# The reciprocal root of a layer norm's variance: one GpSimd power in place of a ScalarE root and a VectorE reciprocal

## The chip, the cores and the metric

The kernel runs on one core of a Trainium2 chip. The metric is the device time of one execution in microseconds. Five engines have instruction streams of their own: TensorE (PE, matmuls), VectorE (DVE), ScalarE (ACT), GpSimd (POOL) and SyncE (SP), which issues nearly all DMAs. Within a stream the order is fixed; between streams the program orders work by semaphores that one instruction raises and another waits for.

## What is computed

The kernel is a two-layer decoder trunk on 256 tokens of width 1024, in float32. Each layer is a token mixer followed by a channel mixer (dense in layer 0, 8 experts with top 2 in layer 1). The change is in the token mixer, in the layer norm of its convolution branch:

```python
def layer_norm(x, g, b):
    mu = jnp.mean(xf, axis=-1, keepdims=True)
    xc = xf - mu
    var = jnp.mean(xc * xc, axis=-1, keepdims=True)
    y = xc * lax.rsqrt(var + LN_EPS) * g + b

def conformer_conv(a, b, dw, dw_b, ln_g, ln_b, w_conv_out):
    u = a * jax.nn.sigmoid(b)
    u = depthwise_conv(u, dw, 31 taps, causal) + dw_b
    u = jax.nn.silu(layer_norm(u, ln_g, ln_b))
    return u @ w_conv_out

def hybrid_mixer(...):
    proj = h @ w_in
    a, b, p, gc, gp = split(proj)
    merged = sigmoid(gc) * conformer_conv(a, b, ...) + sigmoid(gp) * multiscale_pool(p, ...)
    return merged @ w_out
```

The layer norm runs over 512 channels, once in each of the two layers.

## The kernel before

**Weights.** All weights stream from memory in units of 128x2048 float32 (1 MB) into a ring (`raw`). A unit is split for the matmuls into a high part by ScalarE (`w_hi`, L511) and a low part by VectorE (`w_lo`, L765), into three buffers each; a product is three matmuls, high by high (L1108), low by high (L1109) and high by low (L1110). ScalarE may split unit n only when TensorE has finished unit n-3 (`unit_used`). The helper `split_to(n)` puts all splits below n at that place of the engine's stream; U is the first unit of the layer.

**The convolution branch.** It is held transposed, channels on partitions and 256 tokens along a row: `conv` is 128 x (4 chunks x 256), a part of `work`. VectorE and GpSimd sum the 31 taps; GpSimd's additions are the loop over `ADDS` (L450). TensorE then makes the mean over channels by four matmul groups with `mean_w` (L1222), so that every partition holds the mean of each token. VectorE subtracts it (L842), ScalarE squares (L602), and TensorE makes the variance in `bank[7]` (L1228), placed amid the first half of the unit U+12. From there:

- ScalarE takes the square root of variance plus epsilon, 128x256, into `ln_std` (L605).
- VectorE takes the reciprocal into `ln_rstd` (L846) and multiplies all four chunks of `conv` by it (L847), which raises `normed`.
- ScalarE splits unit U+15 and, once `normed` is up, makes for each chunk a sigmoid and an affine map (L610, L611), and after them the fourth block of gate sigmoids (`gate_half(U, 3)`, L552). VectorE multiplies (L852) for the silu, ScalarE and VectorE split the result into `cT_hi` and `cT_lo` (L615, L855).

**TensorE meanwhile** goes through units U+12 and U+13 (gate columns), then the pooling product with unit U+14 for token block 1, and for token block 0 after it, which waits for the gate sigmoids of L552 because they still occupy its banks. Then come the convolution's output product (units U+15, U+16), a transpose, and the output projection.

**GpSimd meanwhile** multiplies the gate block `gate_p` by a row of gains (L459): the two of the left half right after its additions, the two of the right half once L552 has written them. VectorE needs all four (`gate_p_scaled`, L863). In layer 1 the constants of the router follow on GpSimd. It also makes the reciprocal roots of the RMS norms, by a power of a 128x2 tile with the exponent -0.5 held in `small[:, 4:6]` (L402), and of 128x1 tiles at the end (L468).

`ln_std` and `ln_rstd` are halves of the tile `sq`, which the trace calls `work`.

Of the kernel before, what the change touches and what calls it, by code (L numbers as in the profile page):

```python
# [7 lines left out]
ALU = mybir.AluOpType  # L8
ACT = mybir.ActivationFunctionType
# [5 lines left out]
P = 128  # L15
UNIT = 2048
RAW = 7
RMS_EPS, LN_EPS = 1e-6, 1e-5
# [27 lines left out]
def trunk_kernel(nc, x, mix_norm, w_in, conv_dw, conv_dw_b, conv_ln_g, conv_ln_b, w_conv_out, w_pool, pool_scale,  # L46
                 w_out, ffn_norm, dense_w_gate, dense_w_up, dense_w_down, router_w, moe_w_gate, moe_w_up,
                 moe_w_down, final_norm, out):
    _, S, D = x.shape
# [119 lines left out]
    with ExitStack() as ctx:  # L169
        def sb(name, shape, dt=F32):  # L170
            return ctx.enter_context(nc.sbuf_tensor(name, shape, dt))

        def sem(name):
            return ctx.enter_context(nc.semaphore(name))
# [3 lines left out]
        small = sb("small", [P, 16])  # L178
# [79 lines left out]
        ln_std, ln_rstd = sq[:, 0:S], sq[:, S:2 * S]  # L258
# [7 lines left out]
        bank = [ctx.enter_context(nc.psum_tensor(f"bank{i}", [P, N], F32)) for i in range(8)]  # L266
# [21 lines left out]
        prod_ready, prod_added, diag_ready, pe_taps_done = sem("prod_ready"), sem("prod_added"), sem("diag_ready"), sem("pe_taps_done")  # L288
        pooled_done, dT_hi_ready, dT_ready = sem("pooled_done"), sem("dT_hi_ready"), sem("dT_ready")
        mean_done, centred, centred_sq, var_done = sem("mean_done"), sem("centred"), sem("centred_sq"), sem("var_done")  # L290
        std_ready, normed, sig_conv, silu_conv = sem("std_ready"), sem("normed"), sem("sig_conv"), sem("silu_conv")
        cT_hi_ready, cT_ready = sem("cT_hi_ready"), sem("cT_ready")
        yp_merged, yc_gated, merged_ready = sem("yp_merged"), sem("yc_gated"), sem("merged_ready")
# [84 lines left out]
        @block.gpsimd  # L378
        def _(pool):
            seen = Seen(PER_ITEM)  # L380
            steps = [0]

            def step(ins):

                steps[0] += 1
                ins.then_inc(pool_step, 1)
                pool.wait_ge(pool_step, steps[0])


            step(pool.memset(ident[:, :], 0.0))  # L390
            step(pool.affine_select(out=ident[:, :], in_=ident[:, :], compare_op=ALU.not_equal, fill=1.0, base=0,
                                    pattern=[[-1, P]], channel_multiplier=1))
            pool.memset(small[:, 4:6], -0.5)
            pool.memset(small[:, 13:14], LN_EPS)
            pool.memset(uT[:, :, 0:PAD], 0.0)
            step(pool.memset(mean_w[:, :], 1.0 / CD))
            pool.memset(small[:, 12:13], 0.0).then_inc(consts_ready, 1)

            def inverse_root():

                pool.wait_ge(meansq_ready, seen.next(meansq_ready))
                pool.tensor_tensor(small[:, 6:8], small[:, 2:4], small[:, 4:6], ALU.pow).then_inc(rstd_ready, 1)  # L402

            def tap_diagonals(l):
                for j in range(TP):
                    ins = pool.tensor_scalar(diag[:, j, :], ident[:, :], taps[:, l, CC * j + 2:CC * j + 3], None, ALU.mult)  # L406
                ins.then_inc(diag_ready, 1)

            pool.wait_ge(taps_ready, L)
            tap_diagonals(0)  # L410
            inverse_root()

            for g, w in enumerate(WINDOWS):
                pool.memset(band_0[:, g, w - 1:], 1.0 / w)
                for t in range(w - 1):
                    pool.memset(band_0[:, g, t:t + 1], 1.0 / (t + 1))
                step(pool.memset(band_1[:, g, :], 1.0 / w))
                for band, cols in ((band_0, P + REACH), (band_1, P)):
                    step(pool.affine_select(out=band[:, g, :], in_=band[:, g, :], compare_op=ALU.is_ge, fill=0.0, base=0,
                                            pattern=[[1, cols]], channel_multiplier=-1))  # L420
                    step(pool.affine_select(out=band[:, g, :], in_=band[:, g, :], compare_op=ALU.is_ge, fill=0.0,
                                            base=w - 1, pattern=[[-1, cols]], channel_multiplier=1))
                    step(pool.tensor_tensor(band[:, g, 0:P], band[:, g, 0:P], ident[:, :], ALU.subtract))  # L423
            pool.memset(small[:, 12:13], 0.0).then_inc(consts_ready, 1)

            def router_constants():

                step(pool.memset(ones[:, :], 1.0))
                step(pool.affine_select(out=before[:, :], in_=ones[:, :], compare_op=ALU.is_gt, fill=0.0, base=0,
                                        pattern=[[1, P]], channel_multiplier=-1))  # L430
                step(pool.iota(slot_int[:, :], pattern=[[1, P]], base=0, channel_multiplier=0))
                step(pool.tensor_copy(slot_no[:, :], slot_int[:, :]))
                for e in range(E):
                    pool.memset(rev[:, :, e:e + 1], float(E - e))
                    pool.memset(expert[:, e:e + 1], float(e))
                    if e:
                        pool.memset(earlier[:, e, 0:e], 1.0)
                    pool.memset(earlier[:, e, e:E], 0.0)
                pool.memset(slot_of[:, :], NOWHERE)
                step(pool.memset(comb_of[:, :], 0.0))  # L440
                pool.memset(small[:, 12:13], 0.0).then_inc(consts_ready, 1)

            for l in range(L):

                for c, first, n, before_this in ADDS:
                    pool.wait_ge(prod_ready, len(PRODUCTS) * l + n + 1)
                    if before_this:
                        pool.wait_ge(prod_added, len(ADDS) * l + before_this)
                    part = conv[:, c, :] if first is None else tap_prod[:, (len(PRODUCTS) * l + first) % PRODS, :]
                    pool.tensor_tensor(conv[:, c, :], part, tap_prod[:, (len(PRODUCTS) * l + n) % PRODS, :],  # L450
                                       ALU.add).then_inc(prod_added, 1)

                pool.wait_ge(gain_landed, seen.next(gain_landed, 16))
                pool.wait_ge(gates_ready, seen.next(gates_ready, 2 * TB))
                for h in range(2):
                    for b in range(TB):
                        pool.wait_ge(gates_ready, seen.next(gates_ready))
                        part = gate_p[:, b, h * N:(h + 1) * N]
                        pool.tensor_tensor(part, part, row_gain[:, h * N:(h + 1) * N], ALU.mult).then_inc(gate_p_scaled, 1)  # L459
                if l == L - 1:  # L460
                    router_constants()
                inverse_root()
                if l == 0:
                    tap_diagonals(1)
                    inverse_root()
            for b in range(TB):
                pool.wait_ge(meansq_ready, seen.next(meansq_ready))
                pool.tensor_tensor(small[:, 6 + b:7 + b], small[:, 2 + b:3 + b], small[:, 4 + b:5 + b],  # L468
                                   ALU.pow).then_inc(rstd_ready, 1)
# [28 lines left out]
        def _(act):  # L498
            seen = Seen(PER_ITEM)
            unit = [0]  # L500

            def split_to(n):

                while unit[0] < n:
                    u = unit[0]
                    slot, landed, _ = where(u, seen.item is not None)
                    act.wait_ge(raw_landed[slot], seen.at(raw_landed[slot], landed))
                    if u >= SPLIT:
                        act.wait_ge(unit_used, seen.at(unit_used, u - SPLIT + 1))
                    width = unit_width(u)  # L510
                    act.activation(w_hi[:, u % SPLIT, 0:width], place[slot][:, 0:width], ACT.Copy).then_inc(hi_ready, 1)  # L511
                    unit[0] += 1
# [42 lines left out]
            def mixer(l, U):  # L555
# [45 lines left out]
                act.wait_ge(centred, seen.next(centred))  # L601
                act.activation(sq, work[:, 0, :], ACT.Square).then_inc(centred_sq, 1)  # L602
                split_to(U + 15)
                act.wait_ge(var_done, seen.next(var_done))
                act.activation(ln_std[:, :], bank[7][:, 0:S], ACT.Sqrt, bias=small[:, 13:14]).then_inc(std_ready, 1)  # L605
                split_to(U + 16)
                act.wait_ge(normed, seen.next(normed))
                for c in range(CC):
# [138 lines left out]
        def _(dve):  # L747
            seen = Seen(PER_ITEM)
# [3 lines left out]
            def step(ins):  # L752

                steps[0] += 1
                ins.then_inc(dve_step, 1)
                dve.wait_ge(dve_step, steps[0])
# [51 lines left out]
            def mixer(l, U):  # L808
# [27 lines left out]
                bias = vecs[:, V_CB + CC * l + 2:V_CB + CC * l + 3]  # L836
# [5 lines left out]
                dve.tensor_tensor(conv[:, :, :], conv[:, :, :], bank[6][:, 0:S].unsqueeze(1).to_broadcast([P, CC, S]),  # L842
                                  ALU.subtract).then_inc(centred, 1)
                split_to(U + 15)
                dve.wait_ge(std_ready, seen.next(std_ready))
                step(dve.reciprocal(ln_rstd[:, :], ln_std[:, :]))  # L846
                dve.tensor_tensor(conv[:, :, :], conv[:, :, :], ln_rstd[:, :].unsqueeze(1).to_broadcast([P, CC, S]),  # L847
                                  ALU.mult).then_inc(normed, 1)
                split_to(U + 16)
# [570 lines left out]
```

## Time and profile before

| | before |
|---|---|
| device time, median of three runs | 1507.9 us (1507.87 to 1508.37) |
| the profiled execution's device time | 1507.77 us |
| its span in the trace | 1506.0 us |
| layer 0's token mixer | about the first 158 us |
| layer 1's token mixer | about 330 to 485 us |
| TensorE busy | 97% of the span |
| VectorE busy | 79% |
| ScalarE busy | 66% |
| GpSimd busy | 10% |

The span is the time from the first to the last instruction in the trace; the device time of that execution is 1.8 us more. A row of the page's list of groups names a line, an engine, the tiles written and read, their shapes and the count, then the busy time, the mean duration of one and the idle time of the engine just before them. A row of a timeline gives the start in the span, the duration, and in brackets how long the engine was idle before and what ended that.

### The profile page before, as it was taken

The numbers are of one execution on the slowest core, as the hardware profiler recorded it, in microseconds if no ns is written. First come the engines' busy times: TensorE is split into PE (matmuls) and PEld (weight loads), VectorE is DVE, ScalarE is ACT, GpSimd is POOL, SyncE is SP. The second block draws the span as 40 slices with busy tenths as digits, with TensorE's granted clock in tenths as the row PEclk, the third lists the DMA queues.
The fourth block names the chain that finished last, engine by engine and source line by source line (L and its number), as shares of the span: only waits on it lengthen the run. The fifth ranks groups of instructions, "written<-read, shape, count | busy, mean of one in ns | idle before, by whom it ended". The sixth has DMA issues, their size and how long they took to land.

```text
span 1506.0 us, 18439 instructions
## 1 busy us (share of the span) xinstructions
PE 1458.6 (97%) x6617; PEld 1200.0 (80%) x6617; DVE 1193.4 (79%) x979; ACT 993.0 (66%) x880; POOL 152.0 (10%) x236
## 2 busy tenths in 40 slices
PE   7989999999989899999999999999999999999997
PEld 5877888888867688888888888878888888888885
DVE  4767554455867798998899899899889889889986
ACT  5665534435764577767777777776777777777764
POOL 6860400000760000000000000000000000000000
PEclk9999999999999799999999999999999999999999
DMA  9445555555336489999899899998988989999890
GB/s 351 158 139 181 184 182 195 189 175 193 123 117 238 173 324 394 345 341 379 339 357 365 335 364 356 356 385 328 385 346 338 383 333 365 357 356 382 332 369 29
DMA packets 186224, 434.42 MB, mean 288 GB/s; under 512 B 7825, under 2 KB 11201, under 8 KB 186177
## 3 DMA queue, kind: packets, MB, share of 16 engines
q1 hardware_dynamic: 184704, 432.20, 77.1%
q10 hardware_dynamic: 1472, 1.61, 0.3%
q8 instruction: 28, 0.46, 0.1%
q14 instruction: 20, 0.16, 0.0%
HBM read 432.73 MB, written 1.05 MB: 288 GB/s over the span
## 4 chain that ended last, share of the span: by engine, by line
PE 81%; POOL 6%; DVE 4%; issue 4%; ACT 3%; DMA 0%; POOLq 0%; SPq 0%; DVEq 0%; ACTq 0%
PE bank L1108 25%; PE bank L1110 25%; PE bank L1109 25%; POOL work L450 4%; PE bank L1257 2%; ACT w_hi L511 2%; DVE w_lo L765 2%; POOL gates L406 1%; DVE dT_lo L1032 1%; PE bank L1328 1%; PE bank L1353 1%; POOL mix L423 1%; PE bank L1354 0%; DVE xs L892 0%; PE bank L1336 0%
## 5 line engine op out<-in xcount | busy, mean ns | idle before, releaser
L765 DVE TENSOR_TENSOR w_lo<-raw,w_hi 128x2048 fp32r<-128x2048 f32 x315 | 716.9, 2286 | 241.6 <-ACT w_hi L511 240.7
L511 ACT ACTIVATE w_hi<-raw 128x2048 fp32r<-128x2048 f32 x315 | 602.5, 1918 | 361.2 <-PE bank L1110 354.3
L1108 PE MATMUL bank<-w_hi,dT_hi 128*128 128x512 f32 (+1 forms) x912 | 360.7, 395 | 8.2 <-DVE w_lo L765 3.7
L1110 PE MATMUL bank<-w_hi,dT_lo 128*128 128x512 f32 (+1 forms) x912 | 355.0, 389 | 0.0
L1109 PE MATMUL bank<-w_lo,dT_hi 128*128 128x512 f32 (+1 forms) x912 | 354.6, 389 | 0.0
L1108 PE MATMUL bank<-w_hi,cT_hi 128*128 128x512 f32 x568 | 223.4, 393 | 0.0
L1110 PE MATMUL bank<-w_hi,cT_lo 128*128 128x512 f32 x568 | 221.3, 390 | 0.0
L1109 PE MATMUL bank<-w_lo,cT_hi 128*128 128x512 f32 x568 | 221.1, 389 | 0.0
L1108 PEld LDWEIGHTS bank<-w_hi,dT_hi 128*128 128x128 f32 x912 | 172.0, 189 | 47.9 <-issue 6.6
L1110 PEld LDWEIGHTS bank<-w_hi,dT_lo 128*128 128x128 f32 x912 | 171.8, 188 | 36.2
L1109 PEld LDWEIGHTS bank<-w_lo,dT_hi 128*128 128x128 f32 x912 | 172.0, 189 | 33.5
L1108 PE MATMUL bank<-w_hi,hT_hi 128*128 128x512 f32 x464 | 184.7, 398 | 0.7 <-DVE hT_lo L782 0.7
L1109 PE MATMUL bank<-w_lo,hT_hi 128*128 128x512 f32 x464 | 181.9, 392 | 0.0
L1110 PE MATMUL bank<-w_hi,hT_lo 128*128 128x512 f32 x464 | 181.9, 392 | 0.0
L1110 PEld LDWEIGHTS bank<-w_hi,cT_lo 128*128 128x128 f32 x568 | 106.6, 188 | 22.4
L1109 PEld LDWEIGHTS bank<-w_lo,cT_hi 128*128 128x128 f32 x568 | 106.7, 188 | 21.5
L1108 PEld LDWEIGHTS bank<-w_hi,cT_hi 128*128 128x128 f32 x568 | 106.7, 188 | 21.3
L468 POOL TENSOR_TENSOR small<-small 128x1 f32<-128x1 f32 x2 | 2.1, 1036 | 1010.0 <-DVE small L1095 1010.0
L1108 PEld LDWEIGHTS bank<-w_hi,hT_hi 128*128 128x128 f32 x464 | 88.1, 190 | 19.1 <-DVE w_lo L765 1.0
L1110 PEld LDWEIGHTS bank<-w_hi,hT_lo 128*128 128x128 f32 x464 | 87.9, 189 | 18.7
L1109 PEld LDWEIGHTS bank<-w_lo,hT_hi 128*128 128x128 f32 x464 | 88.0, 190 | 18.0
L765 DVE TENSOR_TENSOR w_lo<-work,w_hi 128x2048 fp32r<-128x2048 f32 x32 | 73.4, 2292 | 11.9 <-ACT w_hi L511 11.9
(189 smaller groups left out, 1282.9 us busy)
## 6 DMA issues: line engine op xcount, KB each, us to landing
raw<-in_moe_w_gate_dram SPq DMA_DIRECT2D x96, 1024.0 KB, 7.0
raw<-in_moe_w_up_dram SPq DMA_DIRECT2D x72, 1024.0 KB, 8.7
raw<-in_moe_w_down_dram SPq DMA_DIRECT2D x72, 1024.0 KB, 7.3
raw<-in_w_in_dram SPq DMA_DIRECT2D x28, 1024.0 KB, 5.3
mix<-in_moe_w_up_dram SPq DMA_DIRECT2D x16, 1024.0 KB, 8.8
gates<-in_moe_w_down_dram SPq DMA_DIRECT2D x16, 1024.0 KB, 9.4
gates<-in_moe_w_up_dram SPq DMA_DIRECT2D x16, 1024.0 KB, 9.0
work<-in_moe_w_down_dram SPq DMA_DIRECT2D x16, 1024.0 KB, 9.3
```

The costliest lines, as they stand in the source:

```text
L406: ins = pool.tensor_scalar(diag[:, j, :], ident[:, :], taps[:, l, CC * j + 2:CC * j + 3], None, ALU.mult)
L423: step(pool.tensor_tensor(band[:, g, 0:P], band[:, g, 0:P], ident[:, :], ALU.subtract))
L450: pool.tensor_tensor(conv[:, c, :], part, tap_prod[:, (len(PRODUCTS) * l + n) % PRODS, :], ALU.add).then_inc(prod_added, 1)
L511: act.activation(w_hi[:, u % SPLIT, 0:width], place[slot][:, 0:width], ACT.Copy).then_inc(hi_ready, 1)
L765: dve.tensor_tensor(w_lo[:, u % SPLIT, 0:width], place[slot][:, 0:width], w_hi[:, u % SPLIT, 0:width].bitcast(F32), ALU.subtract).then_inc ...
L1032: dve.scalar_tensor_tensor(tokT_lo[:, k, :], bank[6 + k // 4][:, (k % 4) * P:(k % 4 + 1) * P], vecs[:, g:g + 1], tokT_hi[:, k, :].bitcast( ...
L1108: nc.tensor.matmul(dst, a_hi, b_hi, start=start, stop=False)
L1109: nc.tensor.matmul(dst, a_hi, b_lo, start=False, stop=False)
L1110: return nc.tensor.matmul(dst, a_lo, b_hi, start=False, stop=stop)
L1257: last = nc.tensor.transpose(bank[banks + b][:, f * P:(f + 1) * P], tokP[:, b, f * P:(f + 1) * P], ident[:, :])
L1328: last = nc.tensor.matmul(bank[6 + h][:, :], onehot[:, b, :], part[:, b, h * N:(h + 1) * N], start=b == 0 and part is xn_hi, stop=b == TB ...
L1353: nc.tensor.matmul(bank[banks[h]][:, :], spreadT[:, b, :], y_hi[:, part], start=True, stop=False)
```

## The change

ScalarE's root (L605) goes. VectorE's reciprocal goes as well; in its place VectorE adds epsilon to the variance while it reads it from the bank, and waits. GpSimd, after its additions and before its gate multiplications, raises the 128x256 result to the power -0.5, the exponent read from one column of `small` for all 256 elements. A new semaphore, `ln_root_ready`, tells VectorE to go on with the multiplication.

```diff
@@ gpsimd, in the loop over layers, behind the additions
+                pool.wait_ge(std_ready, seen.next(std_ready))
+                pool.tensor_tensor(ln_rstd[:, :], ln_std[:, :], small[:, 4:5].to_broadcast([P, S]), ALU.pow).then_inc(ln_root_ready, 1)
 
                 pool.wait_ge(gain_landed, seen.next(gain_landed, 16))
                 pool.wait_ge(gates_ready, seen.next(gates_ready, 2 * TB))
@@ scalar
                 split_to(U + 15)
-                act.wait_ge(var_done, seen.next(var_done))
-                act.activation(ln_std[:, :], bank[7][:, 0:S], ACT.Sqrt, bias=small[:, 13:14]).then_inc(std_ready, 1)
                 split_to(U + 16)
@@ vector
                 split_to(U + 15)
-                dve.wait_ge(std_ready, seen.next(std_ready))
-                step(dve.reciprocal(ln_rstd[:, :], ln_std[:, :]))
+                dve.wait_ge(var_done, seen.next(var_done))
+                dve.tensor_scalar(ln_std[:, :], bank[7][:, 0:S], LN_EPS, None, ALU.add).then_inc(std_ready, 1)
+                dve.wait_ge(ln_root_ready, seen.next(ln_root_ready))
                 dve.tensor_tensor(conv[:, :, :], conv[:, :, :], ln_rstd[:, :].unsqueeze(1).to_broadcast([P, CC, S]),
                                   ALU.mult).then_inc(normed, 1)
```

ScalarE's stream from the square (`work<-work 128x1024`) to the sigmoids of layer 0; a table load is an instruction by which the engine fetches the function that the next one uses. Before:

```order
51 L602 ACTIVATE work<-work 128x1024 [waits centred]
52 L511 ACTIVATE w_hi<-raw 128x1024 [waits unit_used,raw_landed0]
53 L605 ACT_TABLE_LOAD
54 L605 ACTIVATE work<-bank,small 128x256 [waits var_done]
55 L511 ACTIVATE w_hi<-raw 128x2048 [waits unit_used,raw_landed1]
56 L610 ACT_TABLE_LOAD
57 L610 ACTIVATE work<-work,vecs 128x256 [waits normed]
58 L611 ACTIVATE work<-work,vecs 128x256
```

And now:

```order
51 L606 ACTIVATE work<-work 128x1024 [waits centred]
52 L515 ACTIVATE w_hi<-raw 128x1024 [waits unit_used,raw_landed0]
53 L515 ACTIVATE w_hi<-raw 128x2048 [waits unit_used,raw_landed1]
54 L612 ACTIVATE work<-work,vecs 128x256 [waits normed]
55 L613 ACTIVATE work<-work,vecs 128x256
```

The root and both table loads beside it are gone, in both layers.

GpSimd's stream behind the additions of layer 0. Before:

```order
57 L450 TENSOR_TENSOR work<-work,tap_prod 128x256 [waits prod_added,prod_ready] x38
58 L459 TENSOR_TENSOR gates<-gates,row_gain 128x512 [waits gates_ready,gain_landed]
59 L459 TENSOR_TENSOR gates<-gates,row_gain 128x512 [waits gates_ready] x3
60 L402 TENSOR_TENSOR small<-small 128x2 [waits meansq_ready]
61 L406 TENSOR_SCALAR gates<-ident,taps 128x128 x16
```

And now:

```order
57 L451 TENSOR_TENSOR work<-work,tap_prod 128x256 [waits prod_added,prod_ready] x38
58 L455 TENSOR_TENSOR work<-work,small 128x256 [waits std_ready]
59 L463 TENSOR_TENSOR gates<-gates,row_gain 128x512 [waits gates_ready,gain_landed]
60 L463 TENSOR_TENSOR gates<-gates,row_gain 128x512 [waits gates_ready] x3
61 L403 TENSOR_TENSOR small<-small 128x2 [waits meansq_ready]
62 L407 TENSOR_SCALAR gates<-ident,taps 128x128 x16
```

The power is one more instruction, ahead of all four gate multiplications. VectorE's stream keeps its length: the reciprocal's place is taken by the addition of epsilon.

## Rows read from the trace of the kernel before

**Rows 1.** The page's first part: busy time, share of span, instructions.
```profile
PE 1458.6 (97%) x6617; PEld 1200.0 (80%) x6617; DVE 1193.4 (79%) x979; ACT 993.0 (66%) x880; POOL 152.0 (10%) x236
```
**Rows 2.** The page's chain that ended last, by engine.
```profile
PE 81%; POOL 6%; DVE 4%; issue 4%; ACT 3%; DMA 0%; POOLq 0%; SPq 0%; DVEq 0%; ACTq 0%
```
**Rows 3.** That chain in order of time, 104 to 120: start, us, what.
```profile
105.25 1.73 PE bank L1228 x8
...
109.81 1.92 ACT w_hi L511
111.73 0.02 issue
111.75 1.28 ACT L610
113.03 0.01 issue
113.04 0.60 ACT work L610
...
117.09 1.16 ACT gates L552 x2
118.24 0.04 issue
118.29 0.39 PE bank L1108
```
**Rows 4.** ACT's timeline, layer 0: start, us, instruction, idle before and its end.
```profile
105.32 1.28 ACT L605 ACT_TABLE_LOAD   x1
107.02 0.48 ACT L605 ACTIVATE work<-bank,small 128x256 f32<-128x256 f32 x1 [0.42 <-PE bank L1228]
```
**Rows 5.** DVE's timeline over the same stretch.
```profile
107.53 1.75 DVE L846 RECIPROCAL work<-work 128x256 f32<-128x256 f32 x1 [0.97 <-ACT work L605]
109.31 1.22 DVE L847 TENSOR_TENSOR work<-work 128x1024 f32<-128x1024 f32 x1
111.76 2.29 DVE L765 TENSOR_TENSOR w_lo<-raw,w_hi 128x2048 fp32r<-128x2048 f32 x1 [1.22 <-ACT w_hi L511]
```
**Rows 6.** PE's timeline: the variance, and the pooling product's two blocks.
```profile
105.09 1.89 PE L1228 MATMUL bank<-work,mean_w 128*128 128x256 f32 x8
...
116.30 0.28 PE L1110 MATMUL bank<-w_hi,dT_lo 128*128 128x256 f32 x1
118.29 0.39 PE L1108 MATMUL bank<-w_hi,dT_hi 128*128 128x256 f32 x1 [1.70 <-ACT gates L552]
```
**Rows 7.** ACT's timeline at the same place of layer 1.
```profile
434.11 0.47 ACT L605 ACTIVATE work<-bank,small 128x256 f32<-128x256 f32 x1
...
440.07 0.60 ACT L610 ACTIVATE work<-work,vecs 128x256 f32<-128x256 f32 x1
```
**Rows 8.** Groups by shape on POOL: shapes, count, busy us, mean ns, idle.
```profile
L450 POOL TENSOR_TENSOR work<-tap_prod 128x256 f32<-128x256 f32 x4 | 2.9, 733 | 25.4 <-ACT tap_prod L543 25.4
L402 POOL TENSOR_TENSOR small<-small 128x2 f32<-128x2 f32 x4 | 2.9, 720 | 252.2 <-DVE small L774 252.2
```
**Rows 9.** The lines of the two powers: duration ns min/median/max.
```profile
L402 POOL TENSOR_TENSOR small<-small x4: 712/718/732, 30.7 to 488.8; 128x2 f32<-128x2 f32 x4
...
L468 POOL TENSOR_TENSOR small<-small x2: 547/1036/1526, 1498.8 to 1500.1; 128x1 f32<-128x1 f32 x2
```
**Rows 10.** The timeline at the kernel's end, the two 128x1 powers.
```profile
1498.84 0.55 POOL L468 TENSOR_TENSOR small<-small 128x1 f32<-128x1 f32 x1 [1009.31 <-DVE small L1095]
...
1499.91 1.27 DVE L1098 SCALAR_TENSOR_TENSOR xs<-xs,small,row_gain 128x1024 f32<-128x1024 f32 x1
1500.07 1.53 POOL L468 TENSOR_TENSOR small<-small 128x1 f32<-128x1 f32 x1 [0.69 <-DVE small L1095]
```
**Rows 11.** POOL's timeline: a 128x2 power and what runs behind it.
```profile
164.53 0.71 POOL L402 TENSOR_TENSOR small<-small 128x2 f32<-128x2 f32 x1 [44.07 <-DVE small L774]
165.22 4.88 POOL L406 TENSOR_SCALAR gates<-ident,taps 128x128 f32<-128x128 f32 x5
```
**Rows 12.** DVE, by line: a 128x256 tensor_scalar that reads a bank.
```profile
L934 DVE TENSOR_SCALAR work<-bank,vecs x4: 475/480/483, 484.7 to 486.3; 128x256 f32<-128x256 f32 x4
```
**Rows 13.** Stretches: length, then PE, PEld, DVE, ACT, POOL busy, PEclk, DMA share, GB/s.
```profile
503.90:509.00 5.10, 5.09 (x12) 4.04 (x13) 2.86 (x9) 1.16 (x3) 0.00 (x0) 0.50 0.63 206
509.00:514.00 5.00, 5.00 (x23) 4.09 (x23) 2.29 (x1) 3.77 (x2) 0.00 (x0) 0.99 0.00 0
```
**Rows 14.** POOL's timeline: the gate multiplications of layer 0.
```profile
100.69 2.50 POOL L459 TENSOR_TENSOR gates<-gates,row_gain 128x512 f32<-128x512 f32 x2
117.74 2.72 POOL L459 TENSOR_TENSOR gates<-gates,row_gain 128x512 f32<-128x512 f32 x2 [14.55 <-ACT gates L552]
```

More of the change, by code:

```diff
@@ L290, in trunk_kernel @@
         mean_done, centred, centred_sq, var_done = sem("mean_done"), sem("centred"), sem("centred_sq"), sem("var_done")
+        ln_root_ready = sem("ln_root_ready")
         std_ready, normed, sig_conv, silu_conv = sem("std_ready"), sem("normed"), sem("sig_conv"), sem("silu_conv")
```

## The prediction

> **What bounds the kernel now.** I read the busy shares first: TensorE is busy for 97% of the span, GpSimd for 10% [rows 1], so a change that does not alter what TensorE does can cost or gain only where TensorE waits. The chain that ended last agrees, with 81% on TensorE and only 3% on ScalarE [rows 2]. The question is therefore whether the root, the reciprocal and the power lie on the chain at the place where they stand. I read the chain in order of time there [rows 3]. It goes from the variance over TensorE's own products to ScalarE's split of the next unit (109.81), then a table load (111.75, 1.28 us), eight sigmoids and affine maps (from 113.04), the gate sigmoids (until 118.25), and back to TensorE at 118.29, which had stood idle for 1.70 us [rows 6]. The root and the reciprocal are not in it. The timelines say why: the root ran from 107.02 to 107.50 [rows 4], the reciprocal from 107.53 to 109.28, the multiplication from 109.31 to 110.53 [rows 5], while ScalarE could not use the result before 113.04. The branch that is changed has 113.04 - 110.53 = 2.51 us of slack. Layer 1 shows the same, from the root at 434.11 to the first sigmoid at 440.07 [rows 7].
>
> **What is removed.** ScalarE loses the root (0.48 us) and two table loads of 1.28 us each. The first load and the root stand where ScalarE would wait anyway, since the split that follows them waits for TensorE until 109.81 [rows 3]. The second load, 111.75 to 113.03, is on the chain. Without it the sigmoids can begin at 111.75, if `normed` is up by then. So the whole removal is worth at most 113.04 - 111.75 = 1.29 us a layer, and TensorE's idle 1.70 us at 118.29 has room for it. Two layers: 2.6 us. VectorE loses the reciprocal, 1.75 us, which hid in the slack.
>
> **What is added on VectorE.** One 128x256 addition that reads a bank. The nearest row is a tensor_scalar of that shape that reads a bank, 0.48 us [rows 12]. The variance is complete at 105.09 + 1.89 = 106.98 [rows 6], so the addition runs until about 107.50, when the root ended before. It costs nothing itself. Queued behind the new wait on VectorE are the multiplication, the split of unit U+15 (2.29 us) and the silu products; the split has its input from 111.73 on and TensorE needs it only behind the stall, so the wait costs what the power costs, once.
>
> **What is added on GpSimd: the term that decides.** The power can begin at about 107.58, when the engine has long finished its left gate multiplications in the old order and, in the new, its additions. Its duration T at 128x256 is not in the trace. The bounds are these. A plain addition of 128x256 takes 0.73 us [rows 8]; a power cannot well be cheaper, so that is the low end. The trace has the same operation at two tiny widths: 128x2 takes 712 to 732 ns, median 718, in four instances, and 128x1 takes 547 ns [rows 9]. The other 128x1 power shows 1.53 us, but it ran against a VectorE instruction with two SBUF inputs from 1499.91 to 1501.18 [rows 10], so I take the undisturbed one. These numbers carry much for their size: two elements of power cost nearly what 256 elements of addition cost. The second element costs 718 - 547 = 171 ns, and 547 - 171 = 376 ns are fixed. If each further element costs as much, T = 547 + 255 x 171 ns = 44.2 us. If nothing were fixed, the highest reading would be 256 x 547 ns = 140 us, which the 128x2 rows already contradict; with the 128x2 row taken as two equal elements behind some 0.13 us of start, (718 - 130) / 2 = 294 ns an element gives 75 us. (The 0.13 us is my estimate of a GpSimd instruction's bare cost from two rows: 0.73 us for an addition of 256 elements and 1.25 us, half of 2.50, for a product of 512 [rows 8, 14], so about 2.0 ns an element and 0.2 us or less fixed.) I take 44.2 us, since both rows of the same operation lie on that line and no row shows a power at a lower price per element.
>
> The Trainium skill, page Perfetto Trace Analysis, section GPSIMD Engine Instruction, says that a GpSimd span in a profile is unreliable and that one should go by the distance between starts. Here the instruction behind a 128x2 power starts 165.22 - 164.53 = 0.69 us after it [rows 11], so at least these rows hold.
>
> **The sum.** The power ends at 107.58 + 44.2 = 151.8. VectorE multiplies for 1.22 us, until 153.05, and ScalarE starts its sigmoids at about 153.1 in place of 113.04: +40.0 us in layer 0. The split of unit U+15 now runs behind the multiplication on VectorE, 2.29 us, while ScalarE is already at the sigmoids; the silu products then start 2.3 us after the sigmoids do, and catch up by the time ScalarE reaches `cT_hi` (4.05 + 1.16 us after the first sigmoid, by rows 3), so nothing is added there. GpSimd's left gate multiplications move from 100.69 to behind the power; they take 2.5 us [rows 14], and the right pair waits for the gate sigmoids 5.2 us after the first sigmoid, as now. No cost. TensorE stands idle from about 116.6 to 158.3. Its granted clock falls in such a pause: after the idle stretch of the router, 12 matmuls of 512 columns took 5.1 us at 0.50, that is at 1.2 GHz, and then 23 took 5.0 us at 0.99 [rows 13]. That costs 5.1 - 12 x 5.0/23 = 2.5 us there; I take 2.3, with 0 and 2.5 as bounds, as the first products here are only 256 columns wide and the one TensorE idle row that I have at this very place, 1.70 us, shows no drop. The removed table load is already in the 40.0. Layer 0: 42.3. Layer 1 has the same distances, root 434.11 and sigmoid 440.07 against 107.02 and 113.04 [rows 7], so 42.3 again. Together +84.6 us on the span of 1506.0: 1590.6, and with the 1.8 us that the device time lies above the span, 1592.4. The median of the runs, 1507.9, is 0.1 above the profiled 1507.77, so I say 1592.5.
>
> Nothing gives this back later. The stall lets the ring of weights fill, but TensorE is the bound behind it, not the DMAs; the seven units are full after a few microseconds, and then SyncE stops too, because VectorE frees no unit while it waits.
>
> **Rivals.** (A) The power is cheap in bulk: the first elements pay a start that the rest do not, and each further element costs what an addition's does, T = 0.73 to 1.2 us. Then `normed` is up at about 110.1, the sigmoids start at 111.75, and each layer gains 1.29 us: 1507.9 - 2.6 = 1505.3, not slower. The point from which this decides is exact: `normed` must be up by 113.04, so the power must end by 113.04 - 1.22 - 0.08 = 111.74, T at most 4.2 us; above it the change loses, below 2.9 us the gain is whole. For it speaks that the trace cannot tell a start from a price per element beyond two elements. Against it: the second element alone cost 171 ns, and under (A) it should have cost a few. The Trainium skill, GPSIMD Engine Reference, section 3.1, gives about 2.6 cycles an element for a two-input operation and about 12 for a body with data-dependent branches; taken as rules for a power they would give 0.6 or 2.6 us by estimate, which is (A). The step between the 128x1 and the 128x2 rows speaks against applying them to a power.
>
> (B) The loop takes several elements at once when it has them, and the tiny tiles see only the remainder path. With four at the price of one, T = 0.4 + 64 x 0.171 = 11.3 us; `normed` at about 120.2, the sigmoids +7.1 us, TensorE idle for 8.8 us and so up to 2.3 us of lower clock: +9.4 a layer, 1507.9 + 18.8 = 1526.7. For it: ordinary in such loops. Against: 128x2 would then rather cost like 128x1 if two were already paired.
>
> (C) The fixed part is smaller than the line says, and the price is the proportional one, T = 75 us: (75 - 4.2) + 2.3 = 73.1 a layer, 1654. For it: only the single undisturbed 128x1 row speaks for 376 ns fixed.
>
> That the change doesn't do what it says is unlikely, as both table loads are gone from the order.
>
> **How the numbers follow.** The forecast 0.62, (B) and what lies between it and the forecast 0.16, (C) 0.12, (A) 0.10. The forecast's own range is T from 38 to 50 us and 0 to 2.5 us for the clock, 1575 to 1605. To hold 8 in 10 the range must reach over (B) and toward (C): 1525 to 1654. A measurement of this kernel can tell about 0.2%, 3.0 us, from no change. (A)'s whole gain is 2.6 us and so inside that; faster by more has 0.02. (A) otherwise, and a T of up to 5.7 us that loses at most 1.5 us a layer, make 0.08 for no change. Slower has 0.90.
>
> **What would show it.** The duration of GpSimd's power at 128x256 is the one number to read first: 44 us by me, 11 by (B), 75 by (C), about 1 by (A). Then ScalarE should show no table load at the sigmoids, and idle until the multiplication; TensorE should be idle at the pooling product's second block until the gate sigmoids for some 41.7 us in place of 1.70, in both layers, with a granted clock of about 0.5 behind it for up to 5 us. Busy time of GpSimd should rise from 152 to about 240 us. I would be wrong if the power's price per element is not what two tiny tiles say; all else hangs on it by subtraction.

## The result and the profile after

The changed kernel takes 1588.1 us (median of four runs, 1586.96 to 1588.64) against 1507.9 (1507.16 to 1508.37): ratio 1.0531, 95% interval 1.0513 to 1.0550, so 5.3% slower, +80.2 us. The forecast was 1592.5. Single executions of one kernel lie up to 5 us apart, so differences of a microsecond are read from the traces. The span of the profiled execution grew from 1506.0 to 1586.3.

The page after, first part, and the chain by engine and line, to be held against [rows 1, 2]:

```profile
PE 1463.2 (92%) x6617; PEld 1203.8 (76%) x6617; DVE 1194.1 (75%) x979; ACT 986.9 (62%) x874; POOL 236.2 (15%) x238
...
PE 76%; POOL 11%; issue 5%; DVE 4%; ACT 2%; DMA 0%; POOLq 0%; SPq 0%; DVEq 0%; ACTq 0%
```

TensorE does the same 6617 matmuls in the same busy time but for 4.6 us; what fell is its share. GpSimd has 84.2 us more. All but 2 us of that are two instructions, the line of the power (count, duration in ns, who waited in us):

```profile
L455 POOL TENSOR_TENSOR work<-work,small x2: 41138/41145/41152, 107.9 to 475.7; 128x256 f32<-128x256 f32 x2
...
who waited for it (us, times):
  DVE work L850: 82.5, 2
```

Layer 0's chain in order of time, after, against [rows 3]: the power, the multiplication, the sigmoids, and TensorE again.

```profile
107.94 41.16 POOL work L455
149.10 0.02 issue
149.12 2.29 DVE work L850
151.41 0.02 issue
151.44 0.60 ACT work L612
...
155.48 1.16 ACT gates L556 x2
156.63 0.04 issue
156.68 0.58 PE bank L1111
```

Both of ScalarE's table loads are gone, as the order said. Its split of unit U+15 ends at 112.15, and the engine then stands for 39.3 us. TensorE stands for 39.7 us in each layer, where it stood for 1.70 [rows 6]:

```profile
156.68 0.58 PE L1111 MATMUL bank<-w_hi,dT_hi 128*128 128x256 f32 x1 [39.67 <-ACT gates L556]
...
524.43 0.58 PE L1111 MATMUL bank<-w_hi,dT_hi 128*128 128x256 f32 x1 [39.67 <-ACT gates L556]
```

Where the 80.3 us of span come from can be read from four starts in each layer: VectorE's subtraction of the mean, the first sigmoid, and the last pair of gate products on VectorE (L869 before, L872 after) that wait for TensorE.

| us | before, layer 0 | after | before, layer 1 | after |
|---|---|---|---|---|
| subtraction starts | 102.04 | 101.28 | 429.54 | 470.72 |
| first sigmoid | 113.04 | 151.44 | 440.07 | 519.19 |
| last gate pair | 130.92 | 172.06 | 457.96 | 538.66 |
| subtraction to sigmoid | 11.00 | 50.16 | 10.53 | 48.47 |
| sigmoid to last gate pair | 17.88 | 20.62 | 17.89 | 19.47 |

The first stretch grew by 39.2 and 37.9, the second by 2.7 and 1.6: 81.4 in all. The span grew by 1.1 less: 0.76 us went ahead of layer 0's subtraction and 0.40 behind layer 1's last gate pair. The 1.2 us by which layer 0's first stretch grew more than layer 1's are TensorE's clock ahead of the variance, which stood low for longer in this execution than in the one before: over 4 us from just ahead of the subtraction the granted clock was 0.50 (100.24 to 104.24), and 0.76 before (101 to 105). It has nothing to do with the power behind it: when the same kernel was executed again, the first stretch took 48.47 us in layer 0 and 48.46 in layer 1.

### The profile page after: what moved, and what is told of

It is laid out like the page before. It is cut to its first block, busy times and chain, and to the rows that moved or that the text cites. A ratio compares the mean times of both kernels' runs of the same rounds, so it can differ in the third digit from the quotient of the medians.

```text
span 1586.3 us, 18435 instructions
## 1 busy us (share of the span) xinstructions
PE 1463.2 (92%) x6617; PEld 1203.8 (76%) x6617; DVE 1194.1 (75%) x979; ACT 986.9 (62%) x874; POOL 236.2 (15%) x238
## 4 chain that ended last, share of the span: by engine, by line
PE 76%; POOL 11%; issue 5%; DVE 4%; ACT 2%; DMA 0%; POOLq 0%; SPq 0%; DVEq 0%; ACTq 0%
PE bank L1111 24%; PE bank L1113 24%; PE bank L1112 24%; POOL work L455 5%; POOL work L451 4%; PE bank L1260 2%; DVE w_lo L767 2%; ACT w_hi L515 1%; POOL gates L407 1%; DVE dT_lo L1035 1%; PE bank L1331 1%; PE bank L1356 0%; PE bank L1357 0%; DVE xs L895 0%; POOL mix L420 0%
## 5 line engine op out<-in xcount | busy, mean ns | idle before, releaser
L1111 PE MATMUL bank<-w_hi,dT_hi 128*128 128x512 f32 (+1 forms) x912 | 361.8, 397 | 84.2 <-ACT gates L556 79.3
L455 POOL TENSOR_TENSOR work<-work,small 128x256 f32<-128x256 f32 x2 | 82.3, 41145 | 13.7 <-DVE work L848 13.7
```

The costliest lines, as they stand in the source:

```text
L455: pool.tensor_tensor(ln_rstd[:, :], ln_std[:, :], small[:, 4:5].to_broadcast([P, S]), ALU.pow).then_inc(ln_root_ready, 1)
L1111: nc.tensor.matmul(dst, a_hi, b_hi, start=start, stop=False)
```

## Experiments

### What a power costs by width

The kernel before, with root and reciprocal kept, and one more power of n columns on GpSimd, which VectorE's multiplication waits for. Nobody reads its result.

```diff
                 pool.wait_ge(gain_landed, ...)          # ahead of this line:
+                pool.wait_ge(std_ready, seen.next(std_ready))
+                pool.tensor_tensor(sq[0:128, 2 * S:2 * S + 16], ln_std[0:128, 0:16], small[0:128, 4:5].to_broadcast([128, 16]), ALU.pow).then_inc(ln_root_ready, 1)
...
                 step(dve.reciprocal(ln_rstd[:, :], ln_std[:, :]))
+                dve.wait_ge(ln_root_ready, seen.next(ln_root_ready))
```

> The kernel before, root and reciprocal kept, with one added power of 128x16 on GpSimd (its result goes where nobody reads it) that VectorE's multiplication waits for. By the straight line through 128x1 (0.547 us) and 128x256 (41.145 us), 159 ns an element: 0.547 + 15 x 0.159 = 2.9 us. If the price per element falls with the width: less at 16 than the line for small widths (171 ns an element, 3.1 us) and visibly under it.

> As the run with 16 columns, with 64. By the line: 0.547 + 63 x 0.159 = 10.6 us. The kernel grows by (10.6 - 0.1) us a layer and up to 2.5 for the clock, less the slack of about 2.5 us that before has there: about 1508 + 2 x 9 = 1526.

> As the run with 16 columns, with 128. By the line: 0.547 + 127 x 0.159 = 20.7 us; the kernel then takes about 1508 + 2 x 20 = 1548.

> As the run with 16 columns, with all 256 columns but only 8 of the 128 partitions. If GpSimd raises all partitions of a column together, the power takes 41 us as with 128 partitions. Rival (it goes through the partitions one after another, so that the price is per number and not per column): half or less, 20 us or under.

The line of the power in the four kernels, in this order (ns, least, median, most):

```profile
L455 POOL TENSOR_TENSOR work<-work,small x2: 2904/2911/2918, 107.3 to 435.7; 128x16 f32<-128x16 f32 x2
```
```profile
L455 POOL TENSOR_TENSOR work<-work,small x2: 10532/10538/10545, 108.3 to 445.6; 128x64 f32<-128x64 f32 x2
```
```profile
L455 POOL TENSOR_TENSOR work<-work,small x2: 20737/20744/20751, 107.5 to 454.8; 128x128 f32<-128x128 f32 x2
```
```profile
L455 POOL TENSOR_TENSOR work<-work,small x2: 41127/41134/41140, 106.5 to 474.1; 8x256 f32<-8x256 f32 x2
```

With the 128x256 power's 41145 ns this is a straight line. From 16 to 64 columns a column costs (10538 - 2911) / 48 = 158.9 ns, from 64 to 128 it costs 159.5, from 128 to 256 it costs 159.4. So a power takes about 0.36 us and 159.4 ns a column, with no discount for width: rival (B) is out, and so are (A) and (C). And 256 columns of 8 partitions take 41.134 us, as those of 128 do: with 8 partitions and with 128 the price is that of the row's length. All four durations came out as expected. Every power here has the exponent -0.5; another exponent was not tried.

The kernels took 1509.3, 1527.7, 1546.8 and 1586.3 us (one run each, 1507.2 for before beside them). The step from 16 to 64 columns, 7.6 us of power a layer, is 9.2 us a layer; from 128 to 256 (on 8 partitions), 20.4 us of power, it is 19.8. What the first step has on top is TensorE's clock. With 16 columns TensorE waits for 1.71 us, as before, and the first sigmoid and the last gate pair are 17.89 us apart; with 64 it waits for 9.1 us, and they are 20.63 and 19.29 us apart. With 256 columns, a wait of 39.8 us, they are 20.32 and 19.22 apart. So in these runs the clock's cost is all there at a pause of 9 us, and a longer one added nothing.

### What is left when the power is cheap

The changed kernel with the power replaced by a product; the reciprocal root is left out.

```diff
-pool.tensor_tensor(ln_rstd[:, :], ln_std[:, :], small[:, 4:5].to_broadcast([P, S]), ALU.pow).then_inc(ln_root_ready, 1)
+pool.tensor_tensor(ln_rstd[:, :], ln_std[:, :], small[:, 4:5].to_broadcast([P, S]), ALU.mult).then_inc(ln_root_ready, 1)
```

> The changed kernel with the power replaced by a product of the same shape and operands; the reciprocal root is left out. My theory (all of the loss is the power's own length and what TensorE's clock does behind the pause it makes; the hand-over itself is free): GpSimd's instruction takes about 0.8 us, ScalarE's sigmoids start when its split ends, the two table loads of each layer are gone, 1.29 us a layer is gained: 1505.3 us. Rival (the hand-over from VectorE to GpSimd and back, or the displaced gate multiplications, cost too): above 1508.

1505.95 us against 1507.42, ratio 0.9985 (0.9976 to 0.9994): between 0.9 and 3.6 us faster, with the expected 2.6 inside. ScalarE's timeline in layer 0 shows what the forecast's rival (A) described, sigmoids directly behind the split and no load between; TensorE's wait went from 1.70 to 0.29 us:

```profile
109.90 1.92 ACT L515 ACTIVATE w_hi<-raw 128x2048 fp32r<-128x2048 f32 x1 [5.54 <-PE bank L1113]
111.72 0.58 ACT L612 ACTIVATE work<-work,vecs 128x256 f32<-128x256 f32 x1
```
```profile
116.96 0.38 PE L1111 MATMUL bank<-w_hi,dT_hi 128*128 128x256 f32 x1 [0.29 <-ACT gates L556]
```

So the hand-over to GpSimd and back is free here, and the loss comes with the power's length: the power itself, and what follows from the pause that it makes. The displaced gate multiplications stood beside VectorE's multiplication in this run too, which took 2.29 us, but it was done by 110.53, before ScalarE's split was. The values behind the layer norm are others in this run; the count of TensorE's matmuls, 6617, is the same.

### The order of GpSimd's work behind the power

In the changed kernel VectorE's multiplication took 2.28 us, where it had taken 1.22 [rows 5], and the split behind it 3.35 in place of 2.29. The left gate multiplications, which the power had pushed behind itself, ran beside them, and took 3.47 us in place of 2.50 [rows 14]:

```profile
149.06 3.47 POOL L463 TENSOR_TENSOR gates<-gates,row_gain 128x512 f32<-128x512 f32 x2
```

The experiment puts them back ahead of the power.

```diff
-                pool.wait_ge(std_ready, ...)
-                pool.tensor_tensor(ln_rstd ..., ALU.pow)
                 for h in range(2):
+                    if h == 1:
+                        pool.wait_ge(std_ready, ...)
+                        pool.tensor_tensor(ln_rstd ..., ALU.pow)
                     for b in range(TB):
```

> The changed kernel with the two left gate multiplications put back ahead of the power. In the trace after, VectorE's multiplication took 2.28 us in place of 1.22 while GpSimd ran these products beside it. If they held each other up, the multiplication is 1.22 us again and each layer is 1.06 us shorter: 1588.1 - 2.1 = 1586.0. Rival (the multiplication is slow for another reason, such as reading what the power has just written): stays at 1588.1 and at 2.28 us.

The multiplication and the split, in the changed kernel and in this one:

```profile
149.12 2.28 DVE L850 TENSOR_TENSOR work<-work 128x1024 f32<-128x1024 f32 x1 [41.27 <-POOL work L455]
151.33 3.35 DVE L767 TENSOR_TENSOR w_lo<-raw,w_hi 128x2048 fp32r<-128x2048 f32 x1
```
```profile
149.46 1.23 DVE L851 TENSOR_TENSOR work<-work 128x1024 f32<-128x1024 f32 x1 [41.26 <-POOL work L460]
150.60 2.28 DVE L768 TENSOR_TENSOR w_lo<-raw,w_hi 128x2048 fp32r<-128x2048 f32 x1
```

The mechanism is settled: alone, both are back at their old length, although the multiplication still reads what the power has just written; beside GpSimd's products each was 1.06 us longer. The times fit turns of one instruction each: the first product ended at 150.32 as if alone (1.26 us) and the multiplication 1.08 us later; the second product ended 1.13 us after the multiplication, and the split about 2.1 us after that. The median does not show the gain. This kernel took 1586.34 us against 1507.42 (ratio 1.0514, 1.0500 to 1.0529). For a closer comparison the changed kernel was run again, unedited.

> The changed kernel itself, unedited, beside the others of this call, so that small differences to it can be read on one chip. 1588.1 us, 80.2 above before; the run with the left gate multiplications ahead of the power gave 1586.3 and the one that keeps TensorE busy 1582.8, so if this one comes out at 1587 to 1589 both steps (about 2 and about 4 to 5 us) stand.

It took 1587.02 against 1508.14 (1.0526, 1.0512 to 1.0540), inside the 1587 to 1589 of the expectation. But each time has to be held against the kernel before beside it, and both are 78.9 us above that: the 2.1 us that were expected don't show in the medians, though the intervals leave room for them. The traces show them (us, layer 0 / layer 1):

| stretch | changed kernel | left gates first | changed, again |
|---|---|---|---|
| subtraction to VectorE's addition | 6.15 / 4.47 | 6.27 / 4.97 | 4.46 / 4.47 |
| addition to first sigmoid | 44.01 / 44.00 | 42.94 / 42.94 | 44.01 / 43.99 |
| sigmoid to last gate pair | 20.62 / 19.47 | 19.59 / 20.54 | 19.41 / 20.37 |

The middle row, in which the power and the multiplication lie, is 1.07 and 1.06 us shorter. The other two, with TensorE's clock ahead of the variance and behind the pause, vary by 1 to 2 us with no edit at all, and that is as much as the gain.

### TensorE's clock behind the pause

```diff
                 for b in reversed(range(TB)):
+                    if b == 0:
+                        for _ in range(170):
+                            nc.tensor.matmul(bank[6][:, :], w_hi[:, s, 0:P], w_hi[:, s, 0:N], start=True, stop=True)
                     pe.wait_ge(gates_ready, seen.next(gates_ready, TB))
```

> The changed kernel with 170 products of 512 columns added on TensorE in the pause of each layer, written to a bank whose contents nobody reads any more. They last 170 x 0.227 = 38.6 us of a pause of 39.7. If the lower clock behind the pause is what made the stretch from the first product to the end of the convolution's output product 2.7 us longer in layer 0 and 1.6 us in layer 1, the time falls by 4.3 us: 1583.8. Rival (that stretch is longer for another reason, such as the later splits): stays at 1588.1.

1582.79 us against 1507.42, ratio 1.0495 (1.0481 to 1.0510): 75.4 above before, where the changed kernel is 78.9 to 80.2 above. So 170 needless products in each pause make the kernel 3.5 to 4.8 us faster. The pause ends at 156.68 in the changed kernel's layer 0; here TensorE starts on the product at 154.58, and the sigmoids began 2.1 us earlier too. The stretches tell why the time falls, first of the changed kernel, then of this one (length, busy us of PE, PEld, DVE, ACT and POOL, granted clock, DMA share, GB/s):

```profile
156.00:161.00 5.00, 4.32 (x16) 4.04 (x17) 4.05 (x6) 4.94 (x8) 2.69 (x2) 0.50 0.57 202
161.00:166.00 5.00, 5.00 (x20) 3.99 (x20) 5.00 (x6) 0.62 (x1) 0.00 (x0) 0.83 0.58 175
```
```profile
156.00:161.00 5.00, 5.00 (x25) 4.16 (x24) 5.00 (x6) 3.37 (x2) 0.75 (x1) 1.00 0.22 87
161.00:166.00 5.00, 5.00 (x24) 4.14 (x23) 5.00 (x7) 1.92 (x1) 0.00 (x0) 1.00 0.74 218
```

After the pause TensorE runs at 1.2 GHz; kept busy, it comes out at 2.4. From the first sigmoid (149.33) to the last gate pair (167.22) it now takes 17.89 us, and 17.89 in layer 1, as before the change (17.88 and 17.89), against 20.62 and 19.47.

### A power of 128x2

The variance is made by a product with equal weights, so every partition holds the same 256 values, and the 128x256 power computes each of them 128 times. As a row's length is what costs, the tokens belong on the partitions. TensorE's product is turned round, so that its result is 128x2; GpSimd raises that; VectorE scales the identity by it; and one more product, with `mean_w`, spreads it over all partitions. (Every element of `mean_w` is 1/512; the factor `CD`, 512, makes up for that.)

```diff
-nc.tensor.matmul(bank[7][:, 0:S], mean_w[:, :], sq[:, c * S:(c + 1) * S], ...)
+nc.tensor.matmul(bank[7][:, b:b + 1], sq[:, c * S + b * P:c * S + (b + 1) * P], mean_w[:, 0:1], ...)   # for both b
...
+dve.tensor_scalar(small[:, 8:10], bank[7][:, 0:TB], LN_EPS, None, ALU.add)
+pool.tensor_tensor(small[:, 10:12], small[:, 8:10], small[:, 4:6], ALU.pow)
+dve.tensor_scalar(sq[:, b * P:(b + 1) * P], ident[:, :], small[:, 10 + b:11 + b], float(CD), ALU.mult, ALU.mult)   # for both b
+nc.tensor.matmul(bank[6][:, 0:S], mean_w[:, :], sq[:, 0:S], start=True, stop=True)   # behind the first unit of U+12
 dve.tensor_tensor(conv, conv, bank[6][:, 0:S] for all chunks, ALU.mult)
```

> The same mathematics with a power of 128x2: TensorE makes the variance with tokens on partitions (128x2 in place of 256 tokens repeated on all 128 partitions), VectorE adds epsilon, GpSimd raises 128x2 to -0.5, VectorE scales the identity by it (two of 128x128), and one TensorE product spreads it to all partitions behind the first unit of U+12. My theory: power 0.72 us, normed by about 111.4 in layer 0's time of before, sigmoids at 111.75 with no table load: 1.29 us a layer gained, 1505.3. Rival (the longer chain over five engines' hand-overs is late and eats the load's gain): 1507 to 1510.

1507.12 against 1507.42, ratio 0.9995 (0.9986 to 1.0004): no change, so the rival was right about the time. VectorE's timeline shows what ate the gain, and it isn't the length of the chain:

```profile
107.52 0.16 DVE L849 TENSOR_SCALAR small<-bank 128x2 f32<-128x2 f32 x1 [1.60 <-PE bank L1237]
108.50 2.54 DVE L852 TENSOR_SCALAR work<-ident,small 128x128 f32<-128x128 f32 x2 [0.82 <-POOL small L455]
111.83 1.22 DVE L855 TENSOR_TENSOR work<-work,bank 128x1024 f32<-128x1024 f32 x1 [0.79 <-PE bank L1243]
```

The two diagonal products stood beside GpSimd's left gate multiplications (108.44 to 110.96) and ended only when those did. From VectorE's addition to the first sigmoid it is now 5.57 us, where it had been 6.02 from the root on, and behind the sigmoids each layer is 0.3 us longer, which was not traced further. The same two engines again, so the same cure, the two left gate multiplications ahead of the power:

> The kernel with the 128x2 power, and the two left gate multiplications put ahead of it. Without that, VectorE's two 128x128 products of the diagonal took 2.54 us beside GpSimd's gate multiplications, in place of 2 x 0.28, and ScalarE's sigmoids started 0.7 us after they could. If the two engines hold each other up there, the diagonal takes 0.6 us, the sigmoids start directly behind ScalarE's split, and the time is 1.29 us a layer under before: 1505.0. Rival (the diagonal is slow for another reason): 2.5 us again and 1507.

```profile
107.15 0.48 DVE L853 TENSOR_SCALAR work<-ident,small 128x128 f32<-128x128 f32 x2 [0.83 <-POOL small L460]
```
```profile
109.04 1.92 ACT L517 ACTIVATE w_hi<-raw 128x2048 fp32r<-128x2048 f32 x1 [4.05 <-PE bank L1119]
110.87 0.58 ACT L614 ACTIVATE work<-work,vecs 128x256 f32<-128x256 f32 x1
```

2.54 us became 0.48, the addition and the first sigmoid are 4.70 us apart, the sigmoids stand directly behind the split, and the kernel takes 1504.88 us against 1508.14: ratio 0.9976, 0.9967 to 0.9985, so 3.3 us under before (2.3 to 5.0 by the interval, with the expected 2.6 inside) and 82 under the change. To see that this gain is the table load and nothing else, a root of 128x1 that nobody reads brings the loads back:

```diff
                 split_to(U + 15)
+                act.activation(small[:, 14:15], small[:, 13:14], ACT.Sqrt, bias=small[:, 13:14])
                 split_to(U + 16)
```

> As the one with the 128x2 power and the left gate multiplications first, plus a root of 128x1 on ScalarE at the old place whose result nobody reads. It brings back the two table loads of each layer and nothing else. If all of the gain is the second load of each layer, it is gone: as before, 1507.5. Rival (the gain comes from the shorter work on VectorE or the shorter variance product): stays near 1505.

1508.03 against 1508.14, ratio 0.9999 (0.9990 to 1.0008): the gain is gone with everything else left in place, so it was the loads. The first of them (104.47 to 105.75) lies in ScalarE's idle time, since the split behind it waits for TensorE; it is the second that counts. The split starts at 110.17 and the sigmoids 3.24 us later, not 1.83:

```profile
110.17 1.92 ACT L517 ACTIVATE w_hi<-raw 128x2048 fp32r<-128x2048 f32 x1 [4.11 <-PE bank L1120]
112.11 1.28 ACT L615 ACT_TABLE_LOAD   x1
113.41 0.60 ACT L615 ACTIVATE work<-work,vecs 128x256 f32<-128x256 f32 x1
```

## Why the prediction was right, step by step

- **The place.** The branch had 2.5 us of slack, and only the second table load was on the chain. Both hold: with a cheap instruction in the power's place the sigmoids came at 111.72, as the page of before had let expect 111.75.
- **The price of the power**, 44.2 us by a line through two tiny tiles, was 41.15. The shape of the line was right; the slope was 159.4 ns and not 171, as it was a difference of two rows of 0.7 and 0.5 us, and 12 ns of error there became 3.05 us over 255 columns. The fixed part is about 0.36 us, near the 0.376 of the estimate. Twice 3.05 is 6.1 us too much. This is the term that was mis-sized most.
- **Gate multiplications moved behind the power: "No cost."** This step failed. They landed beside VectorE's multiplication and made it 1.06 us longer, on the chain, in each layer. The prediction had looked at when their results are needed and not at what they would run beside, although it used a row of just that kind (the second 128x1 power of [rows 10]) to discard a duration. By the same step the limit that it calls exact, T at most 4.2 us, would be about 3.1 with a multiplication of 2.28 us (an estimate; no run had a T between).
- **The sum to the sigmoids.** 40.0 forecast; 40.0 - 3.05 + 1.06 = 38.0, and layer 1 shows 37.9. Layer 0's 39.2 has 1.2 from the clock ahead of the variance.
- **The clock behind the pause**, 2.3 us a layer with 2.5 as the upper bound: 2.7 and 1.6 in the trace, and shown by keeping TensorE busy, which took 3.5 to 4.8 us off the kernel. The 2.7 lies above the bound: in layer 0 the granted clock was 0.50 to 161 and still 0.83 in the 5 us behind that.
- **Nothing given back later.** 81.4 us in the two stretches against 80.3 in the span. Of the difference 0.76 us were gained ahead of layer 0's subtraction, before anything that the edit touches, and 0.40 behind layer 1's last gate pair; whether those 0.40 have to do with the edit is not known.
- **TensorE's idle time**, 41.7 us forecast, was 39.7, by the first two terms.

The terms together: 84.6 forecast, less 6.1 for the slope, plus 2.1 for the multiplication, plus 1.2 for the clock ahead of the variance, less 0.3 for the clock behind the pause, less 1.1 elsewhere, is 80.4; the span grew by 80.3.

Of the rivals, (A) gave the right time for what it assumed (1505.3, and 1505.95 for the cheap instruction in the power's place), and (B) and (C) have no width at which they hold. That the forecast and its range held rests on two rows out of 18439 instructions, and the step that was wrong was covered by the error of the one that was only off in size. That the two errors went opposite ways was luck.

## What to carry to other kernels

Price an instruction on a new shape by rows of the same operation, however small, not by another operation at the same shape: the addition at 128x256 said 0.7 us, the powers at 128x1 and 128x2 said 44. On GpSimd a power pays by the length of its row and not by partitions, so if all partitions hold the same values, turn them so that they lie across the partitions first. And when an instruction is put ahead of others on GpSimd, ask what those will run beside on VectorE.

## What the runs showed of the hardware

- GpSimd's power (exponent -0.5) costs 0.36 us and 159.4 ns a column, from 16 to 256 columns; at 256 columns 8 partitions cost what 128 do. An addition of 256 columns takes 0.73 us [rows 8].
- GpSimd's products of two tiles and VectorE's work between tiles in SBUF hold each other up. A 128x1024 multiplication went from 1.22 to 2.28 us, two products of the 128x128 identity from 0.48 to 2.54, and two 128x512 products of GpSimd from 2.50 to 3.47.
- The power itself took 41.145, 41.144 and 41.144 us in three kernels (the changed one, left gates first, TensorE kept busy), with VectorE and ScalarE idle beside most of it; what it costs beside a busy VectorE is not shown.
- TensorE, given products whose result nobody reads in place of a pause of 39.7 us, had a granted clock of 1.00, 2.4 GHz, through and behind it; without them it comes out at 1.2 GHz, which cost 1.5 to 2.7 us in the four pauses of two executions. A pause of 1.71 us cost nothing, one of 9.1 us 1.4 to 2.7 us.
- A table load on ScalarE, 1.28 us, starts before the wait of the instruction that needs it: the root's began at 105.32, while the root waited for the variance until 107.02 [rows 4]. It costs nothing where the engine waits anyway, and its full length where the engine has just come from other work: of the two loads a layer, only the second was worth anything.
